# Hybrid SSD, differential attention and PEER block: dense blocks' indices for four heads at a time, three buffers for u and v, eight rows moved into the u stage

## The reference

```python
s_half, i_half = lax.top_k(sc, K)                     # sc: (token, head, half, 128), K = 16
cand = s_half[:, :, 0, :, None] + s_half[:, :, 1, None, :]
top_s, top_pos = lax.top_k(cand.reshape(tb, PEER_HEADS, K * K), K)
idx = jnp.take_along_axis(cand_idx, top_pos, axis=-1)
g = jax.nn.softmax(top_s, axis=-1)
h = jax.nn.gelu(jnp.einsum('td,thkd->thk', xb, u[idx]), approximate=False)
out = jnp.einsum('thk,thkd->td', g * h, v[idx])
```

## Time and profile before

| | us |
|---|---|
| median of three runs | 1461.23 |
| profiled execution, its own time | 1465.86 |
| its span | 1464.1 |
| TensorE matmul busy | 1384.9 (95%) |
| VectorE busy | 1124.6 (77%) |
| ScalarE busy | 392.5 (27%) |
| GpSimd busy | 621.6 (42%) |

### The profile page before, as it was taken

One profiled execution on the slowest core, in us unless ns is written; L12 is line 12 of the kernel. 1 busy time (PEld: TensorE's weight loads), 2 busy tenths in 40 slices (PEclk: granted clock), 3 DMA queues, 4 the chain that ended last, 5 costly groups with the idle time before them and its releaser, 6 DMA issues.

```text
span 1464.1 us, 16370 instructions
## 1 busy us (share of the span) xinstructions
PE 1384.9 (95%) x5430; PEld 941.3 (64%) x5430; DVE 1124.6 (77%) x2672; ACT 392.5 (27%) x1073; POOL 621.6 (42%) x516
## 2 busy tenths in 40 slices
PE   7999999997989999999999989999999999999994
PEld 5656647555478888878899879985444444444441
DVE  3445445699889999989999889997777767775667
ACT  3323332334221112012377667672000000000000
POOL 0000000331735542342466656666376755654541
PEclk9999999999999999999999999999999999999997
DMA  6423334773999998798799999999999999999997
GB/s 215 149 90 121 115 136 159 274 280 130 383 364 377 373 331 295 251 381 288 245 387 392 368 366 377 382 380 376 400 374 409 409 410 409 409 410 409 409 409 309
DMA packets 140084, 466.65 MB, mean 319 GB/s; under 512 B 14560, under 2 KB 14944, under 8 KB 139232
## 3 DMA queue, kind: packets, MB, share of 16 engines
q0 software_dynamic: 73728, 268.47, 47.8%
q1 hardware_dynamic: 66272, 197.14, 35.8%
HBM read 461.36 MB, written 4.19 MB: 318 GB/s over the span
## 4 chain that ended last, share of the span: by engine, by line
DVE 33%; DMA 28%; PE 24%; issue 9%; POOL 5%; ACT 1%; SPq 0%; another core or an unknown queue 0%; DVEq 0%; ACTq 0%; POOLq 0%
PE BANKS L597 10%; DMA UV<-v,IDX 9%; DVE X L1371 8%; DMA BIG<-v,IDX 7%; DMA BIG<-u,IDX 6%; PE BANKS L591 6%; DMA UV<-u,IDX 5%; PE BANKS L811 4%; POOL UV L1416 4%; DVE UV L1366 2%; DVE BIG L1366 2%; POOL BIG L1416 2%; DVE BIG L1205 2%; DVE BIG L1197 2%; DVE BIG L1199 1%
## 5 line engine op out<-in xcount | busy, mean ns | idle before, releaser
L1416 POOL DMA_INDIRECT UV<-u,IDX x154 | 186.7, 1212 | 385.7 <-DVE IDX L1256 262.8
L1416 POOL DMA_INDIRECT UV<-v,IDX x156 | 198.6, 1273 | 179.9 <-DVE UV L1366 107.1
L786 PE MATMUL BANKS<-T 128*128 128x256 f32 x1024 | 233.1, 383 | 3.5 <-issue 2.7
L1371 DVE SCALAR_TENSOR_TENSOR X<-UV,HG,X 128x1024 f32<-128x1024 f32 x156 | 200.3, 1284 | 44.8 <-DMA UV<-v,IDX 40.6
L786 PE MATMUL BANKS<-T,Y 128*128 128x256 f32 x1024 | 229.7, 380 | 0.1
L811 PE MATMUL BANKS<-T,BIG 128*128 128x512 f32 x512 | 225.4, 593 | 1.5 <-DVE BIG L1387 1.5
L811 PE MATMUL BANKS<-Y,BIG 128*128 128x512 f32 x512 | 225.1, 592 | 0.0
L1366 DVE SCALAR_TENSOR_TENSOR UV<-UV,Y 128x1024 f32<-128x1024 f32 x154 | 187.0, 1223 | 42.7 <-DMA UV<-u,IDX 41.0
L786 PEld LDWEIGHTS BANKS<-T 128*128 128x128 f32 x1024 | 193.7, 192 | 30.7 <-issue 4.5
L786 PEld LDWEIGHTS BANKS<-T,Y 128*128 128x128 f32 x1024 | 192.6, 191 | 25.5 <-DMA Y<-u_t 0.5
L1416 POOL DMA_INDIRECT BIG<-u,IDX x102 | 120.3, 1180 | 154.6 <-DVE X L1371 50.6
(11 more groups left out here) (255 smaller groups left out, 1204.4 us busy)
## 6 DMA issues: line engine op xcount, KB each, us to landing
T<-u_t SPq DMA_DIRECT2D x64, 512.0 KB
Y<-u_t SPq DMA_DIRECT2D x64, 512.0 KB
T<-v SPq DMA_DIRECT2D x64, 512.0 KB
Y<-v SPq DMA_DIRECT2D x64, 512.0 KB
BIG<-w_in SPq DMA_DIRECT2D x24, 1024.0 KB, 7.3
BIG<-w_q SPq DMA_DIRECT2D x16, 1024.0 KB, 7.9
BIG<-w_out SPq DMA_DIRECT2D x8, 1024.0 KB, 6.1
UV<-v,IDX POOLq DMA_INDIRECT x156
```

What stands on the lines that cost most here:

```text
L786: last = nc.tensor.matmul(PS[i % 4][:, 0:HT], ub[:, c, :], T8[:, 1, c, :], start=(c == 0), stop=(c == KC - 1))
L1371: stt(xb, row, HG[:, n % 2, i % UNIT:i % UNIT + 1], xb, ALU.mult, ALU.add).then_inc(used, 1)
L1416: pool.indirect_dma_start(row_place(s), None, u if kind == "ru" else v, bass.IndirectOffsetOnAxis(IDX[:, b, c:c + 1], 0)).then_inc(row_in[ ...
```

## The change

1. `pick_space` lays out its parts one behind the other for three kinds of unit. The dense blocks (kind 2) work out the keys of four heads in one "y"; for that the one-hot scratch is 1024 wide and lies in Y[:, 3], until now the fourth stream buffer. "y" of a dense block runs at units 9, 11, 13 and 15 only.
2. `STREAM` has three buffers. The waits for the first v loads are written for any number of buffers. With NS = 3 the scores come back before v 3 and x before v 6.
3. In the list `work` eight more rows stand (84 instead of 76); the assumed costs and the pace are new, and the dealing starts 8 us later.
4. Of the scores put away only three of the four parts are written and fetched back, 768 KB.

```diff
-    cost = {"r": 6.2, "y": 5.0, "ru": 1.31, "rv": 1.29, "e": 0.0, "hg": 0.0, "H": 0.2, "w": 0.6, "ws": 1.0, "sel": 0.0, "oh": 1.0}
+    cost = {"r": 4.9, "y": 8.6, "ru": 1.22, "rv": 1.25, "e": 0.0, "hg": 0.0, "H": 0.2, "w": 0.6, "ws": 1.0, "sel": 0.0, "oh": 1.0}
     work = []
-    for n in (8, 9, 10, 11, 12, 13, 14, 15, 4):
-        first, second, keys = pick(n)
-        work += [first] + rows(3) + (on("oh", 0) if n == 4 else []) + [second] + rows(3) + [keys] + rows(2 + n % 2)
+    for n in (9, 11, 13, 15):
+        for q, item in enumerate(many("r", 4 * (n // 2), 4 * (n // 2) + 4)):
+            work += [item] + rows(4)
+            if (n, q) == (13, 1):
+                work += on("ws", 2)
+        work += on("y", n) + rows(3)
         if n in (11, 15):
             work += on("e", n)
-        if n in (12, 4):
-            work += on("ws", 2 + (n == 4))
-        if n == 14:
+        if n == 13:
             work += on("sel", 0)
+    first, second, keys = pick(4)
+    work += [first] + rows(4) + on("oh", 0) + [second] + rows(3) + [keys] + rows(1) + on("ws", 3)
...
-        while w < len(work) and spent < 4.1 * (j + 1):
+        while w < len(work) and spent < 3.44 * (j + 1) - 8:
...
+        def pick_space(kind):
+            nh = 4 if kind == 2 else 2
+            m, place = (KT3[:, :, :].rearrange("p a n -> p (a n)") if kind == 1 else SCR[:, 0:1152]), [0]
...
+            oh = Y[:, NB - 1, :] if kind == 2 else part(HALF)
+            cand = oh[:, 416:416 + NCAND] if kind == 1 else part(NCAND)
...
         STREAM = [T8[:, 0, 0:4, :].rearrange("p c n -> p (c n)"), T8[:, 0, 4:8, :].rearrange("p c n -> p (c n)"),
-                  Y[:, HB, :], Y[:, HB + 1, :]]
+                  Y[:, HB, :]]
...
-        late = lambda n: int(n >= LATE and n < NUNIT)
+        kind_of = lambda n: 2 if n >= NUNIT else int(n >= LATE)
...
-                    sp.dma_start(away, SCA1.rearrange("p a n -> p (a n)")).then_inc(sc_away, 16)
+                    sp.dma_start(away, SCA1[:, 1:4, :].rearrange("p a n -> p (a n)")).then_inc(sc_away, 16)
...
                 if j < NS:
-                    sp.wait_ge(hd_full, NKEY - NS + j + 1)
+                    sp.wait_ge(hd_full, NKEY - (NKEY - 1 - j) % NS)
...
-                        sp.dma_start(SC_BACK.rearrange("p a n -> p (a n)"), away).then_inc(sc_back, 16)
+                        sp.dma_start(SC_BACK[:, 1:4, :].rearrange("p a n -> p (a n)"), away).then_inc(sc_back, 16)
...
+                nh = POS.shape[1]
+                to = slice((q + 1) * UNIT - nh * TOPK, (q + 1) * UNIT)
...
-                o4 = OH.rearrange("p (h k c) -> p h k c", h=2, c=TOPK)
+                o4 = OH.rearrange("p (h k c) -> p h k c", h=nh, c=TOPK)
+                if nh == 4:
+                    dve.wait_ge(ks_done, 16)
```

More of the change, by code:

```diff
@@ L302, in block_program, with part @@
         SQ = KT3[:, :, :].rearrange("p (b a) n -> p b (a n)", b=2)
-        PICK = SCR[:, 0:1152], KT3[:, :, :].rearrange("p a n -> p (a n)")
         SC_BACK = T8[:, 1].rearrange("p c n -> p (c n)").rearrange("p (a n) -> p a n", a=4)
[L306 to L318, removed]
+        def pick_space(kind):
+            nh = 4 if kind == 2 else 2
+            m, place = (KT3[:, :, :].rearrange("p a n -> p (a n)") if kind == 1 else SCR[:, 0:1152]), [0]
+            def part(n):
+                place[0] += n
+                return m[:, place[0] - n:place[0]]
+            oh = Y[:, NB - 1, :] if kind == 2 else part(HALF)
+            cand = oh[:, 416:416 + NCAND] if kind == 1 else part(NCAND)
+            return (oh, cand, part(64 * (kind < 2)).rearrange("p (j k) -> p j k", j=2),
+                    part(nh * TOPK).rearrange("p (h k) -> p h k", k=TOPK),
+                    part(2 * nh * TOPK).rearrange("p (h j k) -> p h j k", j=2, k=TOPK),
+                    part(2 * nh * TOPK).rearrange("p (j k) -> p j k", j=2),
+                    part(nh * TOPK).bitcast(U32).rearrange("p (h k) -> p h k", k=TOPK),
+                    part(2 * nh * TOPK).bitcast(U32).rearrange("p (h j k) -> p h j k", j=2, k=TOPK),
+                    part(5 * nh * TOPK).bitcast(U32).rearrange("p (j k) -> p j k", j=5),
+                    part(nh * TOPK).rearrange("p (h k) -> p h k", k=TOPK))
         KEYS_A = Q2F[:, 0:PH * NKEY].rearrange("p (a n) -> p a n", n=NKEY)
@@ L1209, in choose @@
                 n = b * (PH // 2) + h // 2
-                _, CAND, _, TOPS, _, _, POS, TOPI, _, _ = pick_space(late(n))
-                if late(n):
+                _, CAND, _, TOPS, _, _, POS, TOPI, _, _ = pick_space(kind_of(n))
+                if kind_of(n) == 1:
                     dve.wait_ge(sc_back, 16)
@@ L1215, in choose @@
                 dve.wait_ge(ks_done, b // 2 * 8 + h // 2 * 2 + b % 2 + 1)
-                sc = (SC_BACK if late(n) else SC[b]).rearrange("p a (i n) -> p (a i) n", n=NKEY)
-                top16([(sc[:, 2 * h + j, :], TOPV[:, j, :], TOPI[:, h % 2, j, :]) for j in range(2)])\
+                sc = (SC_BACK if kind_of(n) == 1 else SC[b]).rearrange("p a (i n) -> p (a i) n", n=NKEY)
+                top16([(sc[:, 2 * h + j, :], TOPV[:, j, :], TOPI[:, h % POS.shape[1], j, :]) for j in range(2)])\
                     .then_inc(chosen, 1)
@@ L1224, in choose @@
                 link(last)
-                link(top16([(CAND, TOPS[:, h % 2, :], POS[:, h % 2, :])]))
+                h %= POS.shape[1]
+                link(top16([(CAND, TOPS[:, h, :], POS[:, h, :])]))
             def keys_of_choice(n):
                 b, q = n // 4, n % 4
-                OH, _, ISELU, TOPS, TOPIF, PABF, POS, TOPI, PAB, STEP = pick_space(late(n))
-                g = G[:, b, q * UNIT:(q + 1) * UNIT].rearrange("p (h k) -> p h k", k=TOPK)
-                last = tt(g, TOPS[:, :, :], TOPS[:, :, 0:1].broadcast_to([P, 2, TOPK]), ALU.subtract)
+                OH, _, ISELU, TOPS, TOPIF, PABF, POS, TOPI, PAB, STEP = pick_space(kind_of(n))
+                nh = POS.shape[1]
+                to = slice((q + 1) * UNIT - nh * TOPK, (q + 1) * UNIT)
+                g = G[:, b, to].rearrange("p (h k) -> p h k", k=TOPK)
+                last = tt(g, TOPS[:, :, :], TOPS[:, :, 0:1].broadcast_to([P, nh, TOPK]), ALU.subtract)
                 if n in RAW:
@@ L1242, in keys_of_choice @@
                 link(ts(PAB[:, 2, :], PAB[:, 2, :], 1, None, ALU.bitwise_or))
-                isel = ISELU if b < HB else ISELS[:, b - HB, :, q * UNIT:(q + 1) * UNIT]
+                isel = ISELU if b < HB else ISELS[:, b - HB, :, to]
                 oh = OH.rearrange("p (k c) -> p k c", c=TOPK)
-                o4 = OH.rearrange("p (h k c) -> p h k c", h=2, c=TOPK)
+                o4 = OH.rearrange("p (h k c) -> p h k c", h=nh, c=TOPK)
+                if nh == 4:
+                    dve.wait_ge(ks_done, 16)
                 tt(PAB[:, 3, :], PAB[:, 0, :], PAB[:, 2, :], ALU.bitwise_or)
-                link(tt(oh, bc(PABF[:, 0, :], 2, TOPK), bc(COLS[:, V_FIRST:V_FIRST + TOPK], 1, UNIT), ALU.is_ge))
+                link(tt(oh, bc(PABF[:, 0, :], 2, TOPK), bc(COLS[:, V_FIRST:V_FIRST + TOPK], 1, nh * TOPK), ALU.is_ge))
                 tt(PAB[:, 4, :], pos, PAB[:, 3, :], ALU.bitwise_and)
@@ L1251, in keys_of_choice @@
                 link(nc.vector.reduce_sum(isel[:, 0, :], oh, AXX))
-                link(tt(oh, bc(IOTA[:, 0:TOPK], 1, UNIT), bc(PABF[:, 1, :], 2, TOPK), ALU.is_equal))
+                link(tt(oh, bc(IOTA[:, 0:TOPK], 1, nh * TOPK), bc(PABF[:, 1, :], 2, TOPK), ALU.is_equal))
                 link(tt(o4, o4, bc(TOPIF[:, :, 1, :], 2, TOPK), ALU.mult))
@@ L1453 @@
     args.append(nc.dram_tensor("out", (SEQ, DM), F32, kind="ExternalOutput").ap())
-    args += [nc.dram_tensor(k, (P, 4 * HALF), F32, kind="Internal").ap() for k in ("away", "x_kept")]
+    args += [nc.dram_tensor(k, (P, n * HALF), F32, kind="Internal").ap() for k, n in (("away", 3), ("x_kept", 4))]
     block_program(nc, *args)
```

## The result

The changed kernel takes 1482.83 us (median of four runs, 1476.84 to 1483.84); the kernel before took 1460.54 (1455.20 to 1462.47) on the same chip. The ratio is 1.015, with a 95% interval of 1.0112 to 1.0188. It was forecast slower, at 1468.5 us. The direction holds, and the loss, 22.3 us, is three times the 7.3 of the sum. The time lies outside the 1464 to 1478 of the likeliest case, and inside the whole range (to 1483) by 0.2 us only.

A forecast was written before the change was run, and what follows sets the result against it. Gathered rows and DMA were taken to set the end, with TensorE 14.0 us slack. TensorE's losses of 5.8 (before step 64), 9.2 (seam) and 6.2 (v stage) move "fin" +7.3 us: 1468.5 us from median 1461.23, range 1454 to 1483.

The forecast's parts named there:

- the sum: Whole kernel: TensorE's end 1443.7 + 5.8 + 9.2 + 6.2 = 1464.9, so "fin" starts 7.3 us later.
- the likeliest case: Whole kernel: TensorE's losses exceed its slack and set the end, 1468.5 us, range 1464 to 1478; chance 0.50.
- the rival of slower loads: v stage: loads take 7.2 us, losing 27 us instead of 6.2: 1489; chance 0.12, shared with no saving in "y".
- "Y" and the rows: VectorE before step 64: four-head "y" 9.4 us, saving 8.8; eight rows cost 9.6; net +0.8 us.
- The uncovered wait: Before ru 81: gather 118 reuses the place of ru 80, so VectorE stalls 5.0 us, bounds 2 and 6.
- TensorE's wait at "og" 1: A sign: TensorE's wait for VectorE's "oh" 1 grows from 2.93 us to 8 or so.
- The seam: From u to v: first v loads go out later with three buffers, costing TensorE 9.2 us, bounds 4 and 13.
- The steady v stage: Buffer cycle of 10.45 us against 10.30 needed: 0.15 us lost in each of 41 cycles, 6.2 us.
- The page's rule: Queues take turns, fixed cost about 2.0 us: a load lands in an estimated 4.6 us however many gathers wait.
- The rival that rested on loads in 4.6 us: Loads land in time and rows decide: TensorE ends 1454.9, "fin" moves -2.7 us, 1458.5; chance 0.26.
- its turning point: Rows decide if TensorE loses under 14.0 us in all, leaving 8 us for seam and stage after 5.8.
- The end: Rows end at 1452.4 (1457.6 + 5.8 - 11.0) and no longer matter; TensorE releases "fin" at 1465.0.

The follow-up runs named there:

- the second profile of the kernel before: The kernel before, unchanged, run once more with a profile: 1457.85 us, span 1456.1; the stall around 613 to 633 is gone.
- the first profile: The kernel before, unchanged, in the profile that the prediction read: 1465.86 us, span 1464.1, with a stall around 613 to 633.

## Why the prediction was right in direction and short in size

**The sum and the range.** The direction is right. The size is not: 7.3 us forecast, 22.3 measured. The measured 1482.83 misses the 1464 to 1478 that the forecast gave its likeliest case, and the whole range holds it by 0.2 us, because its upper end was set halfway into the rival of slower loads. But the median load took 6.8 us, not that rival's 7.2. That the range holds is luck.

**"Y" and the rows: right.** A four-head "y" takes 9.28 us (573.83 to 583.11), 9.4 were forecast, its wide instructions 1.22.

**The uncovered wait: right.** GpSimd was released at 594.10 (near 596 forecast), VectorE waited 4.93 us in front of ru 81 (5.0), and opening the place later removes it. Together with the net cost of rows "og" 1 starts 5.0 us later than in the second profile of the kernel before; 5.8 were forecast. Against the first profile it is only 1.2, because that one contains the accident. The sum was made against a profile that carried an extra loss just where VectorE's delay was to appear. TensorE's wait at "og" 1 was to grow to 8 us or so and is 3.83: 5.2 us of waits for u before step 64 stand in its place, and, as forecast, hide in it.

**The seam: right in the main, short by the clock.** From the last one-hot product to v 8 it takes 41.2 us (1002.36 to 1043.56), against 30.8 in the second profile of before: 10.4 lost, 9.2 forecast. v 3 was to land 7.3 us behind its place, and the gap came as told; that the clock falls in it and costs 2.8 us was not in the sum. In exchange the transfer of x was overrated: v 6 was to wait 2.2 us and had no wait (1033.26 + 3.43). Here the slow products 3 and 4 had put off the load of v 6 to 10.3 us behind that of x. But in the trace of three buffers alone it went out 5.1 us behind x, and v 6 waited 0.66.

**The steady v stage: the term that was mis-sized.** I took one latency, 6.72 us, against a lead of 6.86 less 0.3 for the issue, and got 0.15 us in each of 41 cycles, 6.2 us. Measured from v 8 to the end: 431.6 us (1043.56 to 1475.15) against 412.2 in the second profile of before, **19.4 us**, 0.48 in each cycle. The latency was right (median 6.8). The error was to compare a typical latency with the lead as if there were no spread: single loads took 4.3 to 8.6 us. The product that needs a late load waits, and the next early load gives nothing back, since the lead of the next load starts only at the late product's end. The trace bears this out. Read from the starts of the matmuls one by one, 19.6 us are lost between 1040 and 1430: 11.0 in ten delays of 0.7 to 2.0 us at the first matmul of a step, 3.3 in shorter ones at that place, and 5.2 at the second matmul of a step, nearly all of it 0.10 us in each of 50 steps. For eight of the ten the trace has the time of the load that the product waited for, and each of these took 7.5 to 8.6 us. The waits were to be 0.1 to 0.3 us in every third step; more than half of the loss is ten long ones. What makes single loads so late, and why a step's second matmul is late too, stays open. With four buffers 3.43 us more of lead swallow all of it: the same median of 6.8 us, a longest of 8.3, no wait.

**The page's rule.** The Trainium skill (DMA: Bandwidth & Descriptors, "Queues, rings and completion order" and "Anatomy of one DMA") led to an estimate of 4.6 us for a load beside gathers; measured are 6.8 with gathers and 3.4 without. The page fits its fixed cost of about 2.0 us to DMAs that GpSimd issues, and these loads are SyncE's. With 1.3 us for 0.524 MB at 405 GB/s it makes an estimated 3.3 us, and the trace without gathers agrees (3.4). Beside gathers the estimate falls 2.2 us short, and no run separates whether the fixed part grows there or the share of the load is below one half. That the number of waiting gathers does not matter (6.8 us with at most 13 and with at most 8) agrees with turns between the queues. The rival that rested on loads in 4.6 us is out.

That rival also put its turning point wrongly. With TensorE's losses at 14.0 us "fin" stays where it was; but the same sum has the rows end at 1452.4, so they decide only if TensorE (1443.7) loses less than 8.7, which leaves 2.9 us for seam and stage, not 8. By its own 1454.9 TensorE would still have decided.

**The end.** The rows were to end at 1452.4 and ended at 1439.2. Of these 13.2 us, 4.6 are the start ("og" 1 came 1.2 us later than in the first profile, not 5.8). The rest fits TensorE's delays, which leave their bytes to the gathers: when the rows ended, TensorE had 36 us to go and not 12.5, about 7 loads more, by my estimate 9 us at 405 GB/s. It was worth nothing, as TensorE decided. The sum against the first profile, 7.3 us, came out as 17.5 ("fin" 1457.72 to 1475.19). TensorE's end moved by 31.5 us there, where 21.2 were forecast: 1.2 before "og" 1, 0.1 in the second half of u, 10.9 at the seam and 19.3 in the steady stage. Against the second profile it moved by 39.4; the second half of u is 4.6 us shorter in that one, for a reason that no run isolates. The medians say 22.3, since the first profile of before took 4.6 us more than the median then known.

## What to carry to other kernels

Before a stream buffer is given to something else, compare the lead that remains with the loads' time under the traffic of that stage, with the slow loads and not only the typical one, and treat "about equal" as a loss: here a median of 6.8 against a lead of 6.9 us cost 19 us over 120 steps. When scratch is needed for a while only, borrow the buffer for that while: the same change with the fourth buffer returned after step 65 went from 1.5% slower to 0.5% faster, and with one needless wait mended to 0.9% faster (this last step is within the intervals). A new order of steps moves the reuse of a ring's places too, and a place whose last user stands right before its next one is a wait that can be found on paper. A sum that is made against one profile inherits that execution's accidents: a second profile of the kernel before showed a loss of 4 us that was none of the kernel's.

## What was not expected of the hardware

The median time of a 512 KB load doubles from 3.4 to 6.8 us when gathers saturate the DMA engines, and is the same with at most 8 and with at most 13 gathers under way. Its spread is then 4.3 to 8.6 us, and the few slow loads decide. After gaps of 2.8, 1.6, 0.4 and 4.3 us between 1003 and 1024 TensorE's granted clock fell to 0.50 (1.2 GHz) for some microseconds in the changed kernel. It fell at the seam in each other trace with three buffers too, for instance in the one with x fetched late (16 matmuls in 8.64 us) and in the one without late gathers (in 8.80).
